# A decoder layer with retrieved experts: three tiles instead of two block by block at the end, and eight row gathers issued earlier

## What is computed

```python
u = expert_down[idx]
act = jax.nn.gelu(jnp.einsum("pd,ped->pe", xb, u), approximate=False)
coef = gates.reshape(P, PEER_HEADS * K) * act
return jnp.einsum("pe,ped->pd", coef, expert_up[idx])
```

## Time and profile before

| | us |
|---|---|
| median of 3 runs | 1666.71 |
| lowest and highest run | 1664.39, 1669.26 |
| span of the profiled execution | 1662.5 |
| PE busy | 1645.1 (99%) |
| DVE busy | 1177.0 (71%) |
| POOL busy | 914.0 (55%) |
| ACT busy | 683.2 (41%) |
| down stage, last matmul starts | 1132.57 |
| up stage, first matmul starts | 1133.58 |

### The profile page before, as it was taken

The page is one execution under the profiler, slowest core; times in us unless marked ns, Lnnn a source line. Parts: engine busy times, 40 slices in busy tenths (PEclk is TensorE's granted clock), DMA queues, the critical chain, the costliest instruction groups (busy, mean ns, idle before and its releaser), DMA issues.

```text
span 1662.5 us, 25221 instructions
## 1 busy us (share of the span) xinstructions
PE 1645.1 (99%) x7758; PEld 1362.0 (82%) x7758; DVE 1177.0 (71%) x2979; ACT 683.2 (41%) x1029; POOL 914.0 (55%) x723
## 2 busy tenths in 40 slices
PE   9999999999999999999999999999999999999998
PEld 7777889788887888888888888888888888888886
DVE  7867665456896987768777722216888888898886
ACT  5446655533422344343433443323333333333333
POOL 0232242233556666777666766664676776677730
PEclk9999999999999999999999999999999999999999
DMA  9999031332374444444444444459999999999993
GB/s 360 333 416 394 24 92 44 134 115 89 112 250 133 152 144 142 146 139 152 151 136 150 148 139 150 137 192 337 337 379 368 345 391 344 386 357 367 376 342 153
DMA packets 156627, 376.38 MB, mean 226 GB/s; under 512 B 37521, under 2 KB 72849, under 8 KB 153362
## 3 DMA queue, kind: packets, MB, share of 16 engines
q1 hardware_dynamic: 119026, 308.08, 51.8%
q0 software_dynamic: 34816, 67.41, 11.3%
q10 hardware_dynamic: 2720, 0.16, 0.1%
HBM read 312.06 MB, written 63.50 MB: 226 GB/s over the span
## 4 chain that ended last, share of the span: by engine, by line
PE 94%; DVE 2%; DMA 2%; ACT 1%; issue 1%; SPq 0%; DVEq 0%; ACTq 0%
PE bank L1283 17%; PE bank L1285 17%; PE bank L1284 17%; PE bank L1776 10%; PE bank L1780 10%; PE bank L1778 10%; PE bank L1721 1%; DMA g_in<-gate_scratch 1%; PE bank L1367 1%; PE bank L1519 0%; PE bank L1397 0%; PE bank L1323 0%; PE bank L1671 0%; PE bank L1673 0%; PE bank L1672 0%
## 5 line engine op out<-in xcount | busy, mean ns | idle before, releaser
L765 POOL DMA_INDIRECT gate_scratch<-merged,idx_cell x384 | 432.4, 1126 | 213.7 <-issue 110.6
L1283 PE MATMUL bank<-act_hi,whi 128*128 128x512 f32 x1296 | 507.8, 392 | 0.6 <-issue 0.6
L1285 PE MATMUL bank<-act_hi,wlo 128*128 128x512 f32 x1296 | 504.6, 389 | 0.3 <-issue 0.2
L1284 PE MATMUL bank<-act_lo,whi 128*128 128x512 f32 x1296 | 504.5, 389 | 0.2 <-issue 0.2
L2259 DVE TENSOR_TENSOR wlo<-raw,whi 128x1024 fp32r<-128x1024 f32 x247 | 301.9, 1222 | 227.5 <-ACT whi L1191 169.9
L1776 PE MATMUL bank<-whi,chi 128*128 128x512 f32 x768 | 298.8, 389 | 0.6 <-DVE clo L2436 0.6
L1778 PE MATMUL bank<-wlo,chi 128*128 128x512 f32 x768 | 298.8, 389 | 0.0
L1780 PE MATMUL bank<-whi,clo 128*128 128x512 f32 x768 | 298.8, 389 | 0.0
L1283 PEld LDWEIGHTS bank<-act_hi,whi 128*128 128x128 f32 x1296 | 243.5, 188 | 51.1 <-issue 1.6
L1285 PEld LDWEIGHTS bank<-act_hi,wlo 128*128 128x128 f32 x1296 | 243.2, 188 | 51.2 <-issue 0.5
L1284 PEld LDWEIGHTS bank<-act_lo,whi 128*128 128x128 f32 x1296 | 243.4, 188 | 49.9 <-issue 0.5
(11 more groups left out here) (391 smaller groups left out, 1755.3 us busy)
## 6 DMA issues: line engine op xcount, KB each, us to landing
raw<-in_expert_tiles SPq DMA_DIRECT2D x256, 512.0 KB
act_scratch<-aout SPq DMA_DIRECT2D x128, 256.0 KB
gate_scratch<-vbeta SPq DMA_DIRECT2D x24, 1024.0 KB, 18.8
a_in<-act_scratch SPq DMA_DIRECT2D x128, 192.0 KB
g_in<-gate_scratch SPq DMA_DIRECT2D x128, 192.0 KB
raw<-in_in_tiles SPq DMA_DIRECT2D x28, 512.0 KB
modr<-in_mod_tiles SPq DMA_DIRECT2D x24, 512.0 KB
raw<-in_query_tiles SPq DMA_DIRECT2D x16, 512.0 KB
```

The source lines that it names most:

```text
L765: g.indirect_dma_start(out=gate_cells, out_offset=bass.IndirectOffsetOnAxis(ap=idx_cell[:, b, k:k + 1], axis=0), in_=merged[:, b, k:k + 1] ...
L1283: mm(out_bank[:], whi[:, slot, w], act_hi[:, k, :], start=(k == 0), stop=False)
L1284: mm(out_bank[:], whi[:, slot, w], act_lo[:, k, :], start=False, stop=False)
L1285: last = mm(out_bank[:], wlo[:, slot, w], act_hi[:, k, :], start=False, stop=(k == KD - 1))
```

## The change

`LAST` goes from 2 to 3: TensorE takes tiles 125, 126 and 127 block by block. `gather_rows(0)`, the first eight row gathers, with its wait for `s_idx`, moves from behind all scatters to before the scatter of pick 64 of the third block (`ROWS_AHEAD`). The helpers `gather_acts` and `gather_rows` are defined earlier and are otherwise the same.

```diff
-LAST = 2
+ROWS_AHEAD = (2, 64)
+LAST = 3
@@ (gpsimd)
                     if paced[1] > paced[0] or (b, k) == (0, 0):
                         pool.wait_ge(s_act, paced[1])
+                    if (b, k) == ROWS_AHEAD:
+                        pool.wait_ge(s_idx, 1)
+                        gather_rows(0)
                     g.indirect_dma_start(
                         out=gate_cells,
                         out_offset=bass.IndirectOffsetOnAxis(ap=idx_cell[:, b, k:k + 1], axis=0),
                         in_=merged[:, b, k:k + 1], in_offset=None).then_inc(s_sct[q % 2], 16)
...
-            pool.wait_ge(s_idx, 1)
-            gather_rows(0)
             for r in range(2):
                 pool.wait_ge(s_ast[r], 16 * (N_TILES // 2))
             gather_acts(0)
```

More of the change, by code:

```diff
@@ L750, in _ @@
             expert_rows = expert_tiles.rearrange("n p d -> (n p) d")
[L752 to L768, removed]
             def gather_acts(q):
@@ L786, in gather_rows @@
                     ).then_inc(s_rowl[k % ROWS // 2], 16)
-            pool.wait_ge(s_idx, 1)
-            gather_rows(0)
+            gate_cells = gate_flat.unsqueeze(1)
+            pool.wait_ge(s_zst, 16 * FILLS)
+            for b in range(NG):
+                for k in range(PICKS):
+                    if k % MGROUP == 0:
+                        pool.wait_ge(s_mrg, (b * PICKS + k) // MGROUP + 1)
+                    q = (b * PICKS + k) // SGROUP
+                    if k % SGROUP == 0 and q >= 2:
+                        pool.wait_ge(s_sct[q % 2], 16 * SGROUP * (q // 2))
+                    paced = [FIRST_PACED + m * (LAST_PACED - FIRST_PACED) // (NG * PICKS)
+                             for m in (b * PICKS + k - 1, b * PICKS + k)]
+                    if paced[1] > paced[0] or (b, k) == (0, 0):
+                        pool.wait_ge(s_act, paced[1])
+                    if (b, k) == ROWS_AHEAD:
+                        pool.wait_ge(s_idx, 1)
+                        gather_rows(0)
+                    g.indirect_dma_start(
+                        out=gate_cells,
+                        out_offset=bass.IndirectOffsetOnAxis(ap=idx_cell[:, b, k:k + 1], axis=0),
+                        in_=merged[:, b, k:k + 1], in_offset=None).then_inc(s_sct[q % 2], 16)
             for r in range(2):
```

## The result

| | us |
|---|---|
| changed kernel, median of 9 runs (1668.81 to 1677.66) | 1671.6 |
| kernel before, median of 9 runs beside it (1661.98 to 1669.26) | 1666.71 |
| ratio | 1.0039 [1.0023, 1.0055] |
| span of the profiled execution, after / before | 1674.5 / 1662.5 |

The change made the kernel 0.4% slower here, where 0.1% faster was forecast. Runs of either kernel fall in two clusters some 5 us apart (TensorE's mean clock about 0.995 or 0.999; see the end), so where a microsecond matters I compare the runs at 0.999 and above.

A forecast was written before the change was run, and what follows sets the result against it. TensorE, busy 1645.1 of 1662.5 us, was taken as the bound, with gains only at the stage border and tail: -0.78 - 0.67 = -1.45 us, giving 1665.3 us (-0.09%), range 1662.7 to 1668.3.

The forecast's parts named there:

- Border: Between down and up stage: without the gathers the gate load lands earlier and TensorE's wait goes, -0.78 us.
- Tail: End of the run: wider block spacing lets VectorE gate the last block's first half in time, -0.67 us.
- Scatters' slack: GpSimd, third block: 10.1 us of gathers fit into 18.2 us of slack, last scatter stays at 1109.81, 0 us.
- Rival A: Down stage: the gathers hold the scatters up, making it slower, 1667.1 to 1673.1 us; chance 0.07, 0.03 of it past 0.3%.
- Price of the last split: Last tiles: TensorE needs the last tile's split earlier, at 1645.03, but it ends at 1642.53, 0 us.
- Memory: Down stage: gathered rows share bandwidth with tile loads, which run far enough ahead that TensorE sees nothing, 0 us.
- The share of 0.41: Down stage: taking turns by packets would leave the hardware queue 0.41 of 355 GB/s, 146, above its 133.
- The chance of a loss past 0.3%: Whole kernel: the part of the scatter-delay rival's 0.07 that lies past 0.3% slower, put at 0.03.

The follow-up runs named there:

- b1: The changed kernel run again unaltered, beside the kernel before: 1663.03 us, ratio 0.9988.
- e1: The kernel before with only LAST = 3, row gathers left behind the last scatter: 1661.43 us, ratio 0.9992.
- a1: The changed kernel run again unaltered, in another group beside the kernel before: 1669.24 us, ratio 1.0023.
- c1: The changed kernel run again unaltered, in a further group beside the kernel before: 1671.42 us, ratio 1.0037.
- d1: The changed kernel run again unaltered, in the last group beside the kernel before: 1670.88 us, ratio 1.0031.
- d3: The kernel before with LAST = 3 and, at pick 64, eight unused gathers of 128 single values, 4 KB in all: 1670.94 us, ratio 1.0020.
- d2: The kernel before with LAST = 3 and, at pick 64, seven unused plain loads of 512 KB from GpSimd: 1664.85 us, ratio 0.9997.
- c3: The changed kernel with its first eight gathers narrowed to quarter rows, 1.0 MB in all: 1670.69 us, ratio 1.0048.
- d4: The kernel before with only LAST = 3, run once more in another group: 1662.47 us, ratio 0.9993.
- b3: The changed kernel with its eight gathers issued one by one, eight scatters apart: 1659.66 us, ratio 0.9978.
- c2: The changed kernel with its eight gathers issued one by one, run in another group: 1668.45 us, ratio 1.0013.
- a2: The changed kernel with seven more, unused row gathers right behind the eight: 1677.54 us, ratio 1.0073.
- e3: The changed kernel with its eight gathers issued one by one, first run of this variant: 1664.60 us, ratio 0.9995.
- e2: The changed kernel with LAST back at 2, so only the row gathers are moved up: 1663.92 us, ratio 0.9996.

## Why the prediction was wrong

- **Border, -0.78 us: right** in mechanism and size. In after and b1 the starts run on at 0.23 us; in b1 the fourth gate load landed 4.5 us behind its issue, at about 1118 (1121 had been estimated for an issue at 1117.11, and b1 issued it 3.3 us earlier).
- **Tail, -0.67 us: right.** 1.43 us became 0.76, in e1, b1 and after (there the last matmul ends at 1668.80, the sum starts at 1669.56).
- **Scatters' slack, 0 us: right.** The gathers took 10.2 us of GpSimd (1009.48 to 1019.68; 10.1 had been taken) and the last scatter stood at 1123.40, less the 14.1 us shift 1109.3, where it was 1109.81. Rival A had named the right neighbour and the wrong path: the scatters were never late.
- **Price of the last split, 0 us: right.** TensorE has no wait behind 1180 us in any profile with `LAST = 3`.
- **Memory, "0 us": this is the step that failed.** I asked what 4.2 MB do to loads and stores, and answered that well (b1: from 1000 to 1030 the gathers and the tile loads ran side by side and TensorE did not wait). The share of 0.41 took the packets of the earlier trace rows for the units in which queues take turns; no run shows that, and the sum didn't hang on it. I did not ask whether gathers can stop the issue of instructions on an engine that waits for no data. None of the rivals was that, so the range had no room for it. What stood in the sum as 0 us measured 9.3 us in the first profile, 5.0 to 9.2 us for the same kernel in a1, c1 and d1, and nothing in b1. Against that the 1.45 us that were earned are small. The 5.1 us that the first profile lost before 431 us are no part of it.
- **The border of before seemed to vouch for the burst**, since the same eight gathers stood there beside an unbroken TensorE (94 matmuls in 21 us), under the same condition. So did the up stage, where the other gathers run in every kernel and TensorE has no wait under either condition. That gathers are harmless there and not in the down stage I can't explain. At the border GpSimd stood still behind them for 17.6 us; in the new place scatters follow at once. That was not tried.
- **"The chance of a loss past 0.3%: 0.03"** took every engine's waits as caused by this program. The trace of before held the sign against that: the remote waits above, and TensorE itself starting at 506.69, 507.42, 508.11 and 508.83 with "issue" ahead, 0.7 us apart, the same grid, at a loss of 1.9 us.

**What stays open.** What brings the condition about, and by what path gathers reach TensorE's issue. Instruction fetches are seen in the trace as packets of 16 KB and 8 KB on two queues of their own. In after none of 16 KB falls between 454 and 1058 us and none of either kind in the hole (the nearest, of 8 KB, is at 1013.8, and b1 has its like at 1007.2 and no hole); so the 0.70 us steps are not fetches that the trace shows. That a gather's reads of scattered addresses slow some shared path would fit d3 against d2, and c3; it is a guess that no run tests.

## What to carry to other kernels

Judge a step that is moved also by what kind of instruction it puts where, not by its bytes and its engine time alone: here 4 KB gathered by a list cost more than 3.7 MB loaded plainly. Before moving anything into a stretch in which TensorE has no slack, look in the old trace for waits whose releaser the profile can't name; in these 20 profiles every hole came in one that had them. If there are some, a small saving elsewhere (1.5 us here) is a bad trade for a risk of 9. The three tiles alone are the part to keep: e1 and d4 lay 0.7 to 0.8 in a thousand under before, within what these runs can tell from none, with no hole under either condition; the gathers one by one were as fast as the burst where nothing stalled (b3 0.9978 beside 0.9968 to 0.9988) and not clear of a loss where it did (c2 1.0013, with a hole of 4.3 us).

## What the runs showed of the hardware

- TensorE can drop from a start every 0.227 us to one instruction every 0.70 us in the middle of a tile, where the program has no wait, in a loop that had run unbroken for 490 us (after, 1019 to 1029).
- The hole can cost more than itself: in the course of it the clock falls to 1.2 from 2.4 GHz (for 6.8 us in after, 20.5 us in a2, not at all in a1), and where it outlasts the hole the starts are 0.43 us apart.
- A signal of TensorE can reach ScalarE 1.5 to 6.1 us behind the matmul that it tells of (all profiles with remote waits), while TensorE runs on.
- The same lower clock is granted at about 230 us, behind waits of TensorE of 1.2 and 0.8 us in the mixer, for 10.2 us in the profiles of after, a1 and e3 and not at all in those of before, b1 and e2, which have these waits too. Profiles with it leave the mixer at 437 to 439 us, the others at 432.5 to 434.5. That is about what lies between the two clusters of runs, and more than all that the change was to bring.
